# Feature projections of B, AB and C with the high weights multiplied once against u_hi and u_lo side by side

## The reference

```python
def rms_norm(x, gain):
    xf = x.astype(jnp.float32)
    y = xf * lax.rsqrt(jnp.mean(jnp.square(xf), -1, keepdims=True) + EPS)
    return (y * gain.astype(jnp.float32)).astype(x.dtype)

    proj = u @ w_in                                    # ab_mixer: 1,024 by 3,600
    q, f, i, gate = jnp.split(u @ w_in, [...], -1)     # hgrn2_mixer: 1,024 by 4,096
```

## Time and profile before

| | us |
|---|---|
| median of three runs | 954.73 |
| the profiled execution | 953.99 |
| its span (first to last instruction) | 952.4 |
| TensorE busy | 942.1 |
| VectorE busy | 757.2 |
| ScalarE busy | 617.8 |

### The profile page before, as it was taken

The page is one execution under the profiler, slowest core; times in us unless marked ns, Lnnn a source line. Parts: engine busy times, 40 slices in busy tenths (PEclk is TensorE's granted clock), DMA queues, the critical chain, the costliest instruction groups (busy, mean ns, idle before and its releaser), DMA issues.

```text
span 952.4 us, 16792 instructions
## 1 busy us (share of the span) xinstructions
PE 942.1 (99%) x6822; PEld 817.5 (86%) x6822; DVE 757.2 (80%) x1210; ACT 617.8 (65%) x1015; POOL 15.5 (2%) x28
## 2 busy tenths in 40 slices
PE   9999999999999999999999999999999999999997
PEld 7878879989889987887888888899888888888886
DVE  5887678556867998678998888887876689988887
ACT  7566776447767765568766666677456577666665
POOL 0000000000000000000000000004000000000000
PEclk9999999999999999999999999999999999999999
DMA  8734454643253434254566565554545545666562
GB/s 318 243 113 150 136 174 146 221 148 109 91 175 116 151 117 129 89 177 134 176 214 190 194 191 188 195 182 152 158 123 167 155 156 197 201 196 184 194 198 90
DMA packets 44652, 158.03 MB, mean 166 GB/s; under 512 B 4896, under 2 KB 6432, under 8 KB 44576
## 3 DMA queue, kind: packets, MB, share of 16 engines
q1 hardware_dynamic: 43568, 154.29, 50.6%
q0 software_dynamic: 576, 2.10, 0.7%
q10 hardware_dynamic: 432, 0.59, 0.2%
HBM read 155.91 MB, written 1.05 MB: 165 GB/s over the span
## 4 chain that ended last, share of the span: by engine, by line
PE 88%; DVE 7%; ACT 4%; issue 1%; DMA 0%; ACTq 0%; DVEq 0%
PE psum L399 86%; PE psum L408 2%; DVE w_lo L381 2%; DVE feat L1988 1%; ACT w_hi L372 1%; DMA raw<-in_pieces 0%; ACT scr L1054 0%; ACT u_both L630 0%; DVE big L592 0%; ACT feat L1975 0%; DVE scr L3275 0%; DVE x_res L3288 0%; DVE scr L2156 0%; DVE scr L1084 0%; ACT normed L2949 0%
## 5 line engine op out<-in xcount | busy, mean ns | idle before, releaser
L381 DVE TENSOR_TENSOR w_lo<-raw,w_hi 128x1024 fp32r<-128x1024 f32 x287 | 345.9, 1221 | 50.9 <-ACT w_hi L372 50.4
L372 ACT ACTIVATE w_hi<-raw 128x1024 fp32r<-128x1024 f32 x287 | 296.4, 1052 | 43.8 <-PE psum L399 36.9
L399 PE MATMUL psum<-u_both,w_hi 128*128 128x512 f32 x704 | 168.9, 391 | 1.0 <-DVE u_both L621 0.8
L399 PE MATMUL psum<-w_hi,u_hi 128*128 128x512 f32 x400 | 161.4, 404 | 0.5 <-DVE u_lo L641 0.3
L399 PE MATMUL psum<-w_hi,u_lo 128*128 128x512 f32 x400 | 155.9, 390 | 0.0
L399 PEld LDWEIGHTS psum<-u_both,w_hi 128*128 128x128 f32 x704 | 131.0, 188 | 28.5 <-ACT u_both L615 1.2
L399 PE MATMUL psum<-w_lo,u_hi 128*128 128x512 f32 x400 | 123.6, 390 | 0.0
L399 PE MATMUL psum<-u_hi,w_hi 128*128 128x256 f32 x448 | 114.3, 288 | 0.3 <-DVE u_lo L621 0.3
L399 PE MATMUL psum<-u_lo,w_hi 128*128 128x256 f32 x448 | 112.1, 283 | 0.0
L399 PEld LDWEIGHTS psum<-u_both,w_lo 128*128 128x128 f32 x704 | 91.1, 191 | 4.0
L399 PE MATMUL psum<-u_both,w_lo 128*128 128x256 f32 x704 | 92.2, 283 | 0.0
(11 more groups left out here) (331 smaller groups left out, 1182.6 us busy)
## 6 DMA issues: line engine op xcount, KB each, us to landing
raw<-in_pieces SPq DMA_DIRECT2D x287, 512.0 KB, 3.7
post_gain<-in_norm_gains POOLq DMA_DIRECT2D x4, 512.0 KB, 4.5
x_res<-in_x SPq DMA_DIRECT2D x4, 256.0 KB, 5.2
const<-in_table SPq DMA_DIRECT2D x1, 928.0 KB, 6.7
out_x<-x_res SPq DMA_DIRECT2D x1, 512.0 KB, 2.6
cols<-in_cols SPq DMA_DIRECT2D x1, 384.0 KB, 4.8
raw<-in_pieces ACTq DMA_DIRECT2D x1, 256.0 KB, 4.3
raw<-in_pieces SPq DMA_DIRECT2D x1, 256.0 KB, 4.1
```

Of the source, the lines that this page charges most:

```text
L372: act.q.activation(w_hi[i % SPLIT][:, :], raw[i % RAW][:, :], ACT.Copy).then_inc(act.done, act.mark("hi", i))
L381: dve.q.tensor_tensor(w_lo[i % SPLIT][:, :], raw[i % RAW][:, :], w_hi[i % SPLIT][:, :].bitcast(F32), ALU.subtract).then_inc(dve.done, dve. ...
L399: return pe.q.matmul(o, lhs, rhs, start=start, stop=stop, **kw)
```

## The change

- `u_hi` and `u_lo` lie in one tile, `u_pair[:, k, 0]` and `u_pair[:, k, 1]`, so that a matmul can stream 512 columns, 256 of each. `u2_hi` and `u2_lo` become `u2_pair`, in the scratch area.
- For the 12 feature chunks (four each in B, AB and C) `pe_quarter` gives way to `pe_wide_quarter`. Its pieces hold two output blocks and four blocks of input rows: 8 matmuls of 512 columns with `w_hi`, and 8 of 256 with `w_lo`. The products with `u_hi` land in columns 0 to 255 of a bank, those with `u_lo` in 256 to 511. An output block now needs a bank, so a chunk takes all of banks 0 to 3: half 0 (its first two pieces) banks 0 and 1, half 1 banks 2 and 3. The first chunk of a stage takes its pieces in another order (`WIDE_FIRST`).
- A half of chunk c waits until the same half of chunk c-1 is freed.
- Eviction is `dve_wide_half`, three VectorE instructions for a half: copy the `u_lo` sums out, add the `u_hi` sums (this frees the banks), scale in SBUF. They stand at new places in VectorE's order.
- The row of the norm of B lands in bank 4, after `nb2`'s first low part. In AB the gates' `pe_gate_tokens`, and in C the turns of x, stand after the first four matmuls of their piece; they stood after its first 12.
- B's chunks 6 and 7 and all "tokens" chunks keep their form.

```diff
+WIDE = [(0, 0), (0, 1), (1, 0), (1, 1)]
+WIDE_FIRST = [(0, 0), (1, 0), (0, 1), (1, 1)]
...
-    u_t = (sb("u_hi", KT, S, dt=F32R), over_scr("u_lo", SCR - 2048, KT, S))
-    u2_t = (sb("u2_hi", KT, S, dt=F32R), over_scr("u2_lo", SCR - 4096, KT, S))
-    y_t = (u2_t[0], u_t[1])
+    u_pair, u2_pair = sb("u_pair", KT, 2, S, dt=F32R), over_scr("u2_pair", SCR - 4096, KT, 2, S)
+    u_t, u2_t = [(v[:, :, 0, :], v[:, :, 1, :]) for v in (u_pair, u2_pair)]
+    y_t = u2_t
...
+    def pe_wide_quarter(name, c, i, both, u, free=(), free1=(), first=False, between=None):
+
+        n, s = pe_take()
+        hi, lo = (view(w[s], 0, 4, 2, P) for w in (w_hi, w_lo))
+        half, part = (WIDE_FIRST if c == 0 else WIDE)[i]
+        if part == 0:
+            for step in (free, free1)[half]:
+                pe.wait_ge(*step)
+
+        def low(kks):
+            for f in range(2):
+                for kk in kks:
+                    k = 4 * part + kk
+                    last = mm(psum[:, 2 * half + f, 0:S], lo[:, kk, f, :], both[:, k, 0, :], False, k == KT - 1, True)
+            return last
+
+        for pair in range(2):
+            if not first or pair:
+                pe.wait_ge(dve, u, "lo", 2 * part + pair)
+            for f in range(2):
+                for kk in (2 * pair, 2 * pair + 1):
+                    k = 4 * part + kk
+                    if first and pair == 0:
+                        pe.wait_ge(dve, u, "lo", 0, kk)
+                    mm(psum[:, 2 * half + f, :], hi[:, kk, f, :], both[:, k, :, :].rearrange("p a s -> p (a s)"), k == 0,
+                       False, True)
+            if pair == 0 and between:
+                between()
+            if pair == 0 and first:
+                pe_lo(n)
+                low((0, 1))
+        if not first:
+            pe_lo(n)
+        last = low((2, 3) if first else range(4))
+        last.then_inc(pe.done, pe.mark("used", n))
+        if part == 1:
+            pe.also(f"half{half}", name, c)
...
+    def dve_wide_half(name, c, half, dst, scale, norm):
+
+        at, rows = slice(2 * half, 2 * half + 2), dst[:, 2 * half:2 * half + 2, :]
+        dve.wait_ge(dve, "rms_row", norm)
+        dve.wait_ge(pe, f"half{half}", name, c)
+        dve.q.tensor_copy(rows, psum[:, at, S:2 * S]).then_inc(dve.done, dve.mark("copied", name, c, half))
+        dve.wait_ge(dve, "copied", name, c, half)
+        dve.q.tensor_tensor(rows, psum[:, at, 0:S], rows, ALU.add).then_inc(dve.done, dve.mark(f"free{half}", name, c))
+        dve.wait_ge(dve, f"free{half}", name, c)
+        dve.q.scalar_tensor_tensor(rows, rows, scale, rms_row.unsqueeze(1).broadcast_to([P, 2, S]), ALU.mult,
+                                   ALU.mult).then_inc(dve.done, dve.mark(EV[half], name, c))
...
-            before = {0: [[(dve, "Ao", "x0", 0)], [(dve, "Ao", "x0", 1)]],
-                      1: [[(dve, "Ao", "x", 0), (dve, "rms_row", "nb")], [(dve, "Ao", "x", 1)]]
-                      }.get(c) or by_bank(b_evicted(c - 2))
+            before = [[(dve, f"free{half}", "B", c - 1)] if c else [(dve, "Ao", x, t) for t in range(ST)]
+                      for half, x in enumerate(("x0", "x"))]
...
-                pe_quarter("B", c, i, "features", u_t if c < 2 else u2_t, "nb" if c < 2 else "nb2", c % 2, *before)
+                pe_wide_quarter("B", c, i, u_pair if c < 2 else u2_pair, "nb" if c < 2 else "nb2", *before)
...
-                    pe_rms_row("nb", 2, (dve, "Ao", "x", 0))
+                    pe_rms_row("nb", 4, (dve, "nb2", "lo", 0))
...
-            dve_feature_rms("B", c, b_features(c), c % 2, b_scale(c), "nb")
+                if i == 1 and c:
+                    dve_wide_half("B", c - 1, 1, b_features(c - 1), b_scale(c - 1), "nb")
+                elif i == 3:
+                    dve_wide_half("B", c, 0, b_features(c), b_scale(c), "nb")
...
+            free = AB_FREE.get(c) or [[(dve, f"free{half}", "AB", c - 1)] for half in range(2)]
+            pe_wide_quarter("AB", c, i, u_pair, "n00", *free, between=between)
...
         dve_lo()
+        dve_ab_evict(K_, 0)
         dve_u()
         dve_gate_parts()
-        dve_ab_evict(K_)
+        dve_ab_evict(K_, 1)
         dve_lo()
...
+            free = ([(dve, f"free{half}", "C", c - 1)] if c else [(dve, "up_read", 0, FT - 2 + half)] for half in range(2))
+            pe_wide_quarter("C", c, n % 4, u_pair, "n10", *free, first=n == 0, between=pe_c_turns if n == 0 else None)
...
+                dve_wide_half("C", 0, 0, fe[:, heads_of(0), :], 1.0, "n10")
+            elif s == 7:
+                dve_wide_half("C", 1, 0, fe[:, heads_of(1), :], 1.0, "n10")
```

More of the change, by code:

```diff
@@ L185, in quarter, with wide @@
         pieces.append(w[i * PK * P:(i + 1) * PK * P, col:col + NC].reshape(PK, P, NC).transpose(1, 0, 2))
+    def wide(w, first, n, turned=False):
+        for c in range(n):
+            for half, part in WIDE_FIRST if turned and c == 0 else WIDE:
+                col = first + c * NC + half * S
+                pieces.append(w[part * 4 * P:(part + 1) * 4 * P, col:col + S].reshape(4, P, S).transpose(1, 0, 2))
     def chunks(w, first, n):
@@ L212, in weight_pieces @@
     out(a["a_w_out"][0], A_FIRST)
-    chunks(a["w_kv"], 0, 2)
-    chunks(wb, 0, 2)
+    wide(a["w_kv"], 0, 2, True)
+    wide(wb, 0, 2)
     chunks(a["w_kv"], D, 2)
@@ L218, in weight_pieces @@
     for c in (1, 0, 2):
-        chunks(wab, AB_GQKV + c * NC, 1)
-    chunks(wab, AB_MQK, 3)
+        wide(wab, AB_GQKV + c * NC, 1, c == 1)
+    wide(wab, AB_MQK, 1)
+    chunks(wab, AB_MQK + NC, 2)
     chunks(wab, AB_GG, 1)
@@ L223, in weight_pieces @@
     ffn(0)
-    chunks(wc, D, 2)
-    chunks(wc, 0, 2)
+    wide(wc, D, 2, True)
+    wide(wc, 0, 2)
     chunks(wc, 2 * D, 4)
@@ L1816, in ab_evicted @@
         return [(dve, "ev", "AB", c)] if c < 4 else [(act, "ev", "AB", c)] if c > 4 else evicted("AB", c)
-    AB_FREE = {0: [[(dve, "Bo", "x0", 0)], [(dve, "Bo", "x0", 1)]], 1: [[(dve, "Bo", "x", 0)], [(dve, "Bo", "x", 1)]]}
+    AB_FREE = {0: [[(dve, "Bo", x, t) for t in range(ST)] for x in ("x0", "x")], 4: [[(dve, "free0", "AB", 3)]],
+               5: [[(dve, "free1", "AB", 3)]]}
     def pe_ab_quarter(c, i, between=None):
-        free = AB_FREE.get(c) or by_bank(ab_evicted(5 if c == 6 else c - 2))
-        pe_quarter("AB", c, i, "features" if c < 4 else "tokens", u_t, "n00", AB_PAIR[c], *free,
-                   between=between)
+        if c < 4:
+            free = AB_FREE.get(c) or [[(dve, f"free{half}", "AB", c - 1)] for half in range(2)]
+            pe_wide_quarter("AB", c, i, u_pair, "n00", *free, between=between)
+        else:
+            pe_quarter("AB", c, i, "tokens", u_t, "n00", AB_PAIR[c], *(AB_FREE.get(c) or by_bank(ab_evicted(5))),
+                       between=between)
     def act_gate_w():
@@ L1963, in build, with dve_ab_evict @@
     CONV = {K_: (8, "conv_g", 12, 4), Q_: (4, "conv_g", 12, 0), V_: (12, "conv_g", 12, 8), M_: (0, "conv_m", 4, 0)}
-    def dve_ab_evict(c):
+    def dve_ab_evict(c, half):
         if c >= 2:
@@ L1968, in dve_ab_evict @@
             dve.wait_ge(dve, "conv", c - 2)
-        dve_feature_rms("AB", c, raw_cv[c % 2], AB_PAIR[c], 1.0, "n00")
+        dve_wide_half("AB", c, half, raw_cv[c % 2], 1.0, "n00")
     def act_tap3(c):
@@ L2799, in dve_ab @@
         dve_lo()
+        dve_ab_evict(Q_, 0)
         dve_c_row()
@@ L2812, in dve_ab @@
         dve_lo()
+        dve_ab_evict(V_, 0)
         dve_at()
@@ L2821, in dve_ab @@
         dve_level0()
+        dve_ab_evict(M_, 0)
         dve_cm(2)
@@ L3370, in pe_c_quarter @@
         c = n // 4
-        free = [[(dve, "up_read", 0, FT - 2), (dve, "up_read", 0, FT - 1)]] if c < 2 else by_bank(c_evicted(c - 2))
-        pe_quarter("C", c, n % 4, "features" if c < 4 else "tokens", u_t, "n10", c % 2, *free,
-                   first=c == 0 and n % 4 < 1, between=pe_c_turns if n == 0 else None)
+        if c < 4:
+            free = ([(dve, f"free{half}", "C", c - 1)] if c else [(dve, "up_read", 0, FT - 2 + half)] for half in range(2))
+            pe_wide_quarter("C", c, n % 4, u_pair, "n10", *free, first=n == 0, between=pe_c_turns if n == 0 else None)
+        else:
+            free = [[(dve, f"free{c % 2}", "C", 3)]] if c < 6 else by_bank(c_evicted(c - 2))
+            pe_quarter("C", c, n % 4, "tokens", u_t, "n10", c % 2, *free)
     def dve_c_f(g):
         hs = heads_of(g)
-        dve_feature_rms("C", g, fe[:, hs, :], g, 1.0, "n10")
+        dve_wide_half("C", g, 1, fe[:, hs, :], 1.0, "n10")
         dve.wait_ge(dve, "ev", "C", g)
```

15 lines of the change are left out of this document (9 added, 6 removed).

## The result

The changed kernel takes 978.22 us (median of four runs, 977.4 to 978.64) against 954.71 of the kernel before beside it: a ratio of 1.0246, interval 1.0228 to 1.0264. It is 2.5% slower. The forecast was 977.0 with a range of 968 to 986. The profiled execution lasts 977.95 us, its span is 976.2.

The account below looks back on a forecast made before the run. TensorE, busy 942.1 of 952.4 us, was taken as the bound; lags of 2.9 (B), 10.3 (AB) and 8.7 us (C), 5.0 us of savings within, gave 976.6, and a little of the clock 977, range 968 to 986.

Parts of the forecast that it names:

- The saving: TensorE's feature chunks: each of 48 pieces 0.104 us shorter, 5.0 us in all, 1.7 in each stage.
- The eviction: VectorE, per half: copy 0.78, addition 0.69, with scaling 2.2 us; 24 halves add 38 us of its time.
- B: Stage B: TensorE waits 3.4 us at piece 4 and 1.0 at piece 6; stage ends 2.9 us late.
- AB: Stage AB: TensorE 4.8 us late at piece 4, 6.7 at 8, 7.2 at 12, 10.3 at `pe_cx(2)`.
- C: Stage C: TensorE 1.3 us late at piece 4, 7.3 at piece 12, 8.7 by piece 18.
- The sum: All three stages: 2.9 + 10.3 + 8.7 = 21.9 us slower, savings and waits included; median 976.6 us.
- VectorE's way to `pe_cx(2)`: AB: VectorE's queue from `dve_level0`, done at 353.5, through `xx` ends at 363.0 against 352.71; lag 10.3 us.
- four falls: Clock falls at all four waits forecast over 3 us in B, AB and C, none absorbed: 984 to 988 us.
- The clock: TensorE's long waits: falls to half rate cost 1.5 to 3 us each; two not absorbed give 981; chance 0.16.
- the case as summed: Whole kernel: the three stages' lags add up as followed through both queues, 976.6 us; chance 0.72.
- VectorE made up no ground: Rival on VectorE: it makes up unseen ground or the copy is cheap, half the waits go, 960 to 969; chance 0.08.
- The faster case: Rival, all three stages: every half is freed before TensorE comes, no waits, 949.7 us; chance 0.03.

Follow-up runs that it names:

- the kernel with B alone: Wide form in B only, AB and C in the old form, against the kernel before: 957.95 us, ratio 1.0035.
- the kernel with idle matmuls: Changed kernel plus idle matmuls, 34 ahead of piece 4 of AB and 24 ahead of piece 8 of C: 979.97 us, ratio 1.0264 to the kernel before.
- the short eviction: Changed kernel with one VectorE instruction per half, `u_lo` sums left out of the output, every matmul kept: 961.02 us, ratio 1.0071 to the kernel before.
- the last run: Wide form in AB alone, VectorE's order of the changed kernel, ScalarE making the eight copies: 961.36 us, against 966.29 with VectorE's copy.

## Why the prediction was right

- **The saving.** Eight matmuls of 512 columns start within 1.84 us (162.77 to 164.61), 0.230 apart; those of 256 are 0.120 apart ((1.11 - 0.27) / 7). A piece takes 2.80 us (1.84 and 8 x 0.12), for which 2.78 stood in the sum. By these rows the fixed part of a matmul is 0.010 us and the saving 0.08 a piece, a little less than the 0.104 of the sum (16 pieces: 1.3 us for a stage instead of 1.7). The Trainium skill's TensorE: Matmul & The Clock Gate, section "Wait — 56ns, not 53.3ns?", has 2.5 ns; the measurement decides.
- **The eviction.** Its two later instructions start 0.72 us apart, not 0.78, and a half takes 0.72 + 0.72 + 0.61 = 2.05 us, not 2.2. The copy is the one duration for which no row stood, and it came out 0.06 us lower. VectorE's busy time grew by 32.6 us, not 38.
- **B.** Piece 4 starts at 159.89 (159.8 forecast), piece 6 at 166.43 (166.4), the lag is 2.86 (2.9). The wait at piece 4 is 2.90 by the record, where 3.4 were forecast.
- **AB.** Counted from the stage's mark, piece 4 is 4.6 us late (309.01 - 284.75 against 301.43 - 281.75; 4.8 forecast), piece 12 7.0 (7.2), `pe_cx(2)` 10.4 (10.3). Piece 8 waited 0.34 us where 2.3 were forecast, since TensorE came there late from its half rate. The stage ends 11.96 late: 1.2 of the 1.6 us beyond 10.4 are there at 369.7, within the half-rate stretch that starts at 367, and no further wait takes them in. No run has this stage without that fall alone, so its price is read from the trace.
- **C.** With the 14.96 us taken off by which the stage starts late, piece 4 is at 638.5 (638.8 forecast), piece 8 at 652.9 (653.3), piece 12 at 667.5 (667.8); the lag is 8.86 (8.7). The waits at pieces 8 and 12 are 2.97 and 1.91, where over 3 were forecast for both; the second is shorter because half rate had made TensorE late.
- **The sum.** 2.9 + 10.3 + 8.7 = 21.9 forecast, 23.7 measured. The difference is nearly all the one fall. Four sums in the working are slightly off by their own terms, which changes nothing here: the lag at piece 6 of B is 3.8 and not 3.9, VectorE's way to `pe_cx(2)` ends at 363.2 and not 363.0, its round in C is 14.35 us and not 14.5, and four falls give 983 to 989 and not 984 to 988. The clock stood as a rival of its own, with a chance of 0.16 and 1.5 to 3 us for a fall. Its mechanism is there, with three falls, two of them at waits that were forecast over 3 us; what was argued against it, that the next wait for VectorE takes a fall in, held for two of the three. On the median the sum was 976.6 and the forecast 977.0, and the result lies 1.6 above the sum. So the case as summed came true, with a piece of the clock's on top of it.
- **The rivals.** VectorE made up no ground where the chain says that it was the bound. The faster case turned on whether half 0 is free at 156.45 in B; it was free at 159.8. It did come true in B once the halves stood elsewhere, by 1.2 us in that stage.

What the experiments add is the cause behind the waits. In AB it is for the most part VectorE's time: at the same places, 2.05, 1.33 and 0.6 us for a half give lags of 11.9, 7.6 and 4.7. The last 4.7 stay although VectorE has no more to do than before; how much of them is the banks' and how much half rate's was not taken apart. In B the place in VectorE's order is enough (2.9 to -1.2 us with nothing shortened), and the length counts too (about 1.1 by the estimate above). In C both count, with the length ahead (8.9 to 1.1 us when the half is short, 8.9 to 5.4 when it is moved); what holds C at 5 us after the move was read from waits and not tried.

## What to carry to other kernels

Wide matmuls save TensorE the fixed part of a matmul, here 0.08 us in a piece of 2.88, but an output block then holds twice the banks, and another engine must add up its sums: before taking them, ask when the engine that frees a bank comes to it in its own order, and what it has to do until then. Where that engine has idle time the change is worth its small gain once the evictions are placed well; where it is busy 19 of 20 us, as in AB, 4.4 of the 5.8 us taken off it came back. A predicted wait on TensorE as long as these should be priced with a fall of the clock, some 1.5 us here, which is free only if another wait for the same engine follows.

## What had not been expected of the hardware

- The clock's fall isn't tied to the length of the wait alone. A wait of 2.90 us at piece 4 of B had no fall in the changed kernel and one in the kernel with B alone, and in the kernel with idle matmuls, which is the same up to there, a wait of 2.91 had one. A wait of 2.18 us had one, and in C waits of 2.95 (none) and 2.97 us differ in the same way. In the kernel with every copy made by ScalarE one came at a wait of 1.42 us, ahead of which stood six matmuls of four columns, and one at a wait of 2.02, while in the kernel with ScalarE's copies in B and C alone a wait of 2.04 had none. Each half-rate stretch inside the kernels lasted 3.41 us, or 6.83 as in the short eviction and in the last run.
- ScalarE copies 128 x 512 sums from PSUM in 0.57 us (L649), VectorE in 0.68 (L652). The faster engine was the worse place wherever its order brought it there late.
- VectorE's instruction that needs the result of the one ahead starts 0.11 us later than one that doesn't: 0.72 against 0.61 us for 512 columns.
